# Two more blocks of seven products in a float32 transformer kernel: the per-layer gate's last two units, and the final norm in two halves

## The reference

```python
    y = _rms(h, norm_ple_g[i])
    h = h + jax.nn.sigmoid(y @ w_ple_gate[i]) * (p[i] @ w_ple_proj[i])
return _rms(h, final_norm_g)
...
x = x + swa_sink_mixer(rms_norm(x, swa_norm[idx]), swa_w_in[idx], ...)
```

## Time and profile before

| | |
|---|---|
| median of 3 runs | 1376.66 us (1376.61 to 1378.14) |
| the profiled execution | 1376.73 us |
| its span, first to last instruction | 1375.0 us |
| PE busy | 1369.3 us, 6169 instructions |
| DVE busy | 1156.1 us (84%) |
| ACT busy | 885.2 us (64%) |
| POOL busy | 151.3 us (11%) |
| mean granted TensorE clock | 1.000 |

### The profile page before, as it was taken

The page is one execution under the profiler, slowest core; times in us unless marked ns, Lnnn a source line. Parts: engine busy times, 40 slices in busy tenths (PEclk is TensorE's granted clock), DMA queues, the critical chain, the costliest instruction groups (busy, mean ns, idle before and its releaser), DMA issues.

```text
span 1375.0 us, 16935 instructions
## 1 busy us (share of the span) xinstructions
PE 1369.3 (100%) x6169; PEld 1122.6 (82%) x6169; DVE 1156.1 (84%) x1332; ACT 885.2 (64%) x1181; POOL 151.3 (11%) x129
## 2 busy tenths in 40 slices
PE   9999999999999999999999999999999999999998
PEld 7888888888888888888888888888888887777887
DVE  5589986687999988899999889988766769886898
ACT  7476755576777555777756576756666656665554
POOL 2000010011111000111100011100000144430000
PEclk9999999999999999999999999999999999999999
DMA  9776648887999788999987889998987878889686
GB/s 329 252 212 216 201 158 283 278 242 241 296 279 261 234 257 253 271 269 265 281 262 251 254 253 244 284 290 241 310 312 270 278 242 260 257 265 281 210 251 174
DMA packets 183146, 352.93 MB, mean 257 GB/s; under 512 B 13105, under 2 KB 37933, under 8 KB 182936
## 3 DMA queue, kind: packets, MB, share of 16 engines
q1 hardware_dynamic: 160408, 291.66, 64.5%
q0 software_dynamic: 9568, 35.02, 13.2%
q10 hardware_dynamic: 13088, 25.18, 6.1%
HBM read 296.19 MB, written 27.31 MB: 235 GB/s over the span
## 4 chain that ended last, share of the span: by engine, by line
PE 99%; DVE 0%; DMA 0%; ACT 0%; issue 0%; SPq 0%
PE acc L2216 14%; PE acc L2397 14%; PE acc L2400 14%; PE acc L2399 14%; PE acc L2217 14%; PE acc L2218 14%; PE sp L2400 2%; PE sp L2399 2%; PE tp L2400 2%; PE tp L2399 2%; PE sp L2397 2%; PE tp L2397 2%; PE acc L2278 1%; PE sp L2517 1%; PE tp L2533 1%; PE tp L2236 0%
## 5 line engine op out<-in xcount | busy, mean ns | idle before, releaser
L979 ACT ACTIVATE w_hi<-w_raw 128x1024 fp32r<-128x1024 f32 x451 | 472.1, 1056 | 294.8 <-PE acc L2218 188.0
L1419 DVE TENSOR_TENSOR w_lo<-w_raw,w_hi 128x1024 fp32r<-128x1024 f32 x429 | 519.1, 1225 | 131.6 <-ACT w_hi L979 128.7
L2216 PE MATMUL acc<-w_lo,hh 128*128 128x512 f32 x480 | 189.0, 394 | 0.0
L2218 PE MATMUL acc<-w_hi,hl 128*128 128x512 f32 x480 | 186.9, 389 | 0.0
L2217 PE MATMUL acc<-w_hi,hh 128*128 128x512 f32 x480 | 186.9, 389 | 0.0
L2397 PE MATMUL acc<-w_lo,yh 128*128 128x512 f32 x452 | 176.0, 389 | 0.0
L2399 PE MATMUL acc<-w_hi,yh 128*128 128x512 f32 x452 | 175.9, 389 | 0.0
L2400 PE MATMUL acc<-w_hi,yl 128*128 128x512 f32 x452 | 175.9, 389 | 0.0
L979 ACT ACTIVATE w_hi<-wide 128x1024 fp32r<-128x1024 f32 x108 | 114.3, 1060 | 69.6 <-DVE wide L1433 30.2
L1419 DVE TENSOR_TENSOR w_lo<-wide,w_hi 128x1024 fp32r<-128x1024 f32 x108 | 131.5, 1222 | 14.9 <-ACT w_hi L979 14.6
L2216 PE MATMUL acc<-w_lo,yh 128*128 128x512 f32 x352 | 137.4, 390 | 0.0
(11 more groups left out here) (333 smaller groups left out, 2227.6 us busy)
## 6 DMA issues: line engine op xcount, KB each, us to landing
w_raw<-in_w_gate SPq DMA_DIRECT2D x88, 512.0 KB, 5.8
w_raw<-in_w_up SPq DMA_DIRECT2D x88, 512.0 KB, 6.2
w_raw<-in_w_down SPq DMA_DIRECT2D x88, 512.0 KB, 6.4
w_raw<-in_w_in SPq DMA_DIRECT2D x64, 512.0 KB, 4.6
wide<-w_raw POOLq DMA_DIRECT2D x54, 512.0 KB, 5.9
w_raw<-in_swa_w_in ACTq DMA_DIRECT2D x48, 512.0 KB, 5.2
w_raw<-in_w_out SPq DMA_DIRECT2D x32, 512.0 KB, 5.8
w_raw<-in_w_ple_gate SPq DMA_DIRECT2D x32, 512.0 KB, 6.6
```

The source lines that it names most:

```text
L979: act.activation(w_hi[:, v % SPL], src, ACT.Copy).then_inc(hi_ready, 1)
L1419: dve.tensor_tensor(w_lo[:, v % SPL], src, w_hi[:, v % SPL].bitcast(F32), ALU.subtract).then_inc(lo_ready, 1)
L2216: pe.matmul(dst, xh[:, f, tk], w_lo[:, v % SPL, k], start=(f == 0), stop=False)
L2218: last = pe.matmul(dst, xl[:, f, tk], w_hi[:, v % SPL, k], start=False, stop=(f == CK * end + CK - 1))
```

## The change

Units 2 and 3 of the per-layer gate become one block (`PLE_PAIR`) with twenty entries: twelve plain chunks and two sets of `g`, `u`, `t`, `s`, for chunks 0 and 1 of both units. Its activation sums are made in the earlier part of the stage (`p_whole_sum`, `sum_p`, their high part on ACT, their low part on DVE). The sums of weights lie in `p_weights`, over parts of `hh` and `hl` that are not yet in use. The results of units 2 and 3 now come through DVE (`sum_third_gate` adds what `mix` left to the PSUM banks) and then through the sigmoid (`gate_third`). The loads of the projection are issued earlier. The moves of the first two columns to the second layer (`T_SWA`, `T_SWA + 1`) are both issued after the block's tenth load; before, one load and two further loads stood ahead of them. `SWA_STEPS` now takes four chunks of unit 0, four of unit 1, then the rest. The final norm's two instructions are set at two different chunks, each counted by itself.

```diff
-UNITS += [(8, "a")] * 4
+UNITS += [(8, e) for e in "aadd"]
...
-PLE_ORDER += [(j, c) for j in (2, 3) for c in range(8)]
...
+PLE_PLAN = plain(0, 2, 3) + quad("g", 0) + plain(0, 4) + quad("g", 1) + plain(0, 5) + plain(1, 2, 3) + quad("u", 0)
+PLE_PLAN += quad("t", 0) + quad("s", 0) + quad("u", 1) + plain(1, 4) + quad("t", 1) + quad("s", 1) + plain(0, 6, 7)
+PLE_PLAN += plain(1, 5, 6, 7)
+PLE_AT = dict(taken=(1, 3), turned=(2, 4), low=(7, 12), m1=13, mix=16, sum=18, pool_low=17,
+              copied={3: [0], 4: [1]}, summed={0: 7, 1: 11})
+PLE_PAIR = Block(PLE_UNIT + 2, PLE_PLAN, **PLE_AT)
...
-                if n in (13, 16, 19, 22):
-                    fetch_proj((13, 16, 19, 22).index(n))
-                if n == 26:
+                if n in (11, 14):
+                    fetch_proj((11, 14).index(n))
+            b = PLE_PAIR
+            for i, p in enumerate(b.loads):
+                role = int(p[0] == "u" or p[:2] == ("n", 1))
+                load(b.raw + i, wpg_v, CK * p[-1], CW * (2 + role))
+                if i in (4, 8):
+                    fetch_proj((4, 8).index(i) + 2)
+                if i == 9:
                     move(T_SWA, freed=T_PLE + 2)
-                if n == 28:
                     move(T_SWA + 1, freed=T_PLE + 3)
...
+            b = PLE_PAIR
+            for i in range(len(b.plan)):
+                for q in b.at["copied"].get(i, ()):
+                    copy_tops(b, q)
+                split_high(b.v0 + i)
+                if i in b.at["taken"]:
...
+                    take(PLE_UNIT + j, tok(0), ACT.Sigmoid, rp)
+                if i in b.at["turned"]:
...
+                    square(3, j, junk=1)
+                if i in b.at["low"]:
+                    swa_turned_high(b.at["low"].index(i))
+                if i == b.at["m1"]:
+                    copy_m1(b)
...
+            b = PLE_PAIR
+            for i in range(len(b.plan)):
+                if i != b.at["pool_low"]:
+                    split_low(b.v0 + i)
+                if i in b.at["taken"]:
+                    add_gated(b.at["taken"].index(i))
+                if i in b.at["turned"]:
+                    turn_gated(b.at["turned"].index(i))
+                if i in b.at["low"]:
+                    swa_turned_low(b.at["low"].index(i))
+                if i == b.at["mix"]:
+                    mix(b)
+                if i == b.at["sum"]:
+                    sum_third_gate(0)
...
-                        for t in range(T):
-                            last = dve.scalar_tensor_tensor(resid[:, t], resid[:, t], rs[:, R_FIN, t:t + 1], big[:],
-                                                            ALU.mult, ALU.mult)
-                        last.then_inc(x1_ready, 1)
...
+                        dve.scalar_tensor_tensor(resid[:, c], resid[:, c], rs[:, R_FIN, c:c + 1], big[:],
+                                                 ALU.mult, ALU.mult).then_inc(x1_ready, 1)
```

More of the change, by code:

```diff
@@ L335, in build @@
             h_wide_front = first.enter_context(nc.sbuf_tensor("h_wide", [P, PAIRS_OF_DOWN, 4, P], F32))
+        with ExitStack() as first:
+            p_weights = []
+            for i in range(2):
+                first.enter_context(nc.sbuf_tensor(f"front{i}", [P, 8, S], F32))
+                p_weights.append(first.enter_context(nc.sbuf_tensor(f"p_weights{i}", [P, 4, CW], F32)))
         hh, hl = sb("hh", [P, KT, S], F32R), sb("hl", [P, KT, S], F32R)
```

149 lines of the change are left out of this document (98 added, 51 removed).

## The result

The changed kernel took 1381.41 us (median of 7 runs, 1380.30 to 1382.71), the kernel before, run beside it, 1376.88 us (7 runs): a ratio of 1.0027, 95% interval 1.0017 to 1.0037. It is slower, by 4.5 us between the medians, where 1.5 us were forecast. The median lies 0.6 us above the end of the forecast range (1380.8); the ratio, laid on the 1376.66 us of before, gives 1380.4, just inside. The profiled execution is the longest of the seven, 1382.71 us, 5.98 us over the profiled one of before.

The account below looks back on a forecast made before the run. PE was taken to bound the kernel, so every matmul removed and every PE wait counts: 1376.73 - 1.36 (six matmuls) + 2.8 (waits in the block) = 1378.2 us. The range was 1375.3 to 1380.8.

Parts of the forecast that it names:

- Six matmuls, -1.36 us: In the block, two sets of 21 matmuls replace 2 x 24, six fewer at 0.2267 us each: 1.36 us less.
- First place, sixth entry, 0.7: At the block's sixth entry, DVE's split is ready at 1028.45, wanted at 1027.8; PE waits about 0.7 us.
- Second place, the load at the thirteenth entry: The load waits for raw slot and SP's list, landing at 1039.2; PE starts at 1041.7 instead of 1040.0.
- The accumulating transfer is no limit: issued at about 1021.1, landed 5.9: POOL's transfer for the sums, in the block: landed 5.9 us after issue, wanted only past 1030, so no wait.
- Third place, `t` 1: At the fourteenth entry, the second column's parts stand between splits; PE starts at 1045.5 instead of 1042.8.
- The three places together, 2.8: Waits at the block's sixth, thirteenth and fourteenth entries together make PE 2.7 to 2.8 us late; 2.8 taken.
- The projection's earlier loads ... nothing, and at worst the 1.2 us of one instruction: First half of the stage: earlier projection loads and activation sums cost nothing, at worst 1.2 us.
- the 8.0 us of the slowest load in the stage: Loads behind the thirteenth entry's: even at 8.0 us to landing their chunks are in time.
- all first loads behind a fetch stayed at 5.0 or less: Argument against the late-load rival: first loads behind a fetch landed in 5.0 us or less.
- The second layer at nothing: Second layer's start: third and fourth columns and the final norm in halves are in time; cost nothing.
- The rival of a late load: Thirteenth entry's load lands in up to 8.0 us, fourteenth entry 6.1 us late, time 1381.5; chance 0.12.
- The quick load: Thirteenth entry's load lands at 1037.5, fourteenth entry only 1.1 us late, time 1376.5; chance 0.13.

Follow-up runs that it names:

- e2: Changed kernel with ACT's two copies for the sums of weights at the block's first and third entries, not fourth and fifth; 3.29 us of waits in the block.
- e3: Changed kernel with the second column's high and low parts at the block's fifteenth entry instead of its thirteenth, behind `s` 1; median 1383.00 us.
- n1: The kernel before with only its final norm in two halves; stage 87.04 us, rest to the last matmul 310.70 us.
- e1: Changed kernel with the projection's four fetches back where they stood before; median 1381.35 us against 1381.41.
- e4: Changed kernel with three loads between the two column moves, as before the change; median 9.3 us over that of the changed kernel.
- e11: e10 with the bias rows' loads back behind GpSimd's scale for the second layer; times 1376.36 to 1382.32 us.
- e5: Changed kernel with both first-pair sets behind five plain products and the moves behind the eleventh and twelfth loads; stage 88.95 us.
- e10: e9 with the keys' last two products ahead of the second unit's chunk 4; stage 86.96 us, rest 310.69 us, one run at 1375.99.
- e9: e6 with bias rows issued ahead of POOL's next scale and the sums' copies one entry earlier; stage 86.29 us.
- e6: e5's order and moves, plus earlier copies, low parts at `(7, 16)` and projection fetches as before, on the changed kernel; stage 86.47 us, time same as before.

## Why the prediction was wrong in its size

The side and the kind of mechanism were right: slower, with waits that eat the gain of the six matmuls. The size was not, 4.5 us for 1.5; the forecast had given a time above 1379.4 a chance of 0.16. By its steps:

- *Six matmuls, -1.36 us*: right; 186 matmuls in the block.
- *First place, sixth entry, 0.7*: 0.77, and gone with earlier copies (e2).
- *Second place, the load at the thirteenth entry*: right in place, cause and landing (4.6 for 4.7), but 2.43 us where 1.0 were forecast. It failed in one step, the sentence "The accumulating transfer is no limit: issued at about 1021.1, landed 5.9". I asked only when that transfer itself is wanted. What it does to the fetch beside it I left at the rows of a stretch without one: 2.7 us a piece became 6.2. That puts the high part, the last sum, the slot and so the load some 2.2 us later, and makes a wait before `t` 0 that stood nowhere in the walk. The trace of before had a row that could have warned me, the fetch issued at 975.75 us, beside a transfer of 1024 KB from POOL's queue:

```profile
tile<-parked SPq DMA_DIRECT2D x4, 128.0 KB, 6.6
```

- *Third place, `t` 1*: 1.07 us for 1.1, and its cause as forecast (e3).
- *The three places together, 2.8*: 4.89 us in the changed kernel, 3.29 in e2, where no accumulating transfer is beside the fetch. The 3.29 are near 2.8 in part by luck, with one put 1.0 us longer and the other 1.6 us shorter than the 4.2 priced.
- *"The projection's earlier loads ... nothing, and at worst the 1.2 us of one instruction"*: 1.7 us of wait before unit 2 in the profile of the changed kernel, none there in the four others with that order. I looked for cover on DVE and ACT and not in the DMA queue, though the row that it rests on has a DMA share of 0.98. That step is incomplete in any case: the fetch took 8.9 to 13.9 us for 5.3 to 6.8, and only the column's slack hid it from PE in four of five.
- *"the 8.0 us of the slowest load in the stage"* and *"all first loads behind a fetch stayed at 5.0 or less"*: both misread. In the trace of before a load issued at 982 us took 11.4, and the load of 8.0 us, issued at 978.30, is itself the first behind a fetch. The result does not hang on it, since the load in question took 4.6.
- *The second layer at nothing*: right for the columns and for the cutting of the norm in halves (2.35 us each at 1084.20 and 1087.60, no late split; n1). Wrong for `SWA_STEPS` and for the norm's later place, which holds up the bias rows: 0.42 us together. I asked when the inputs come and not who waits for the first unit's result.
- *The rival of a late load*, 1381.5 us, met the time, but not by its mechanism: it has a slow landing of the load (up to 8.0 us), which took 4.6. *The quick load*, on the side of the page "DMA: Bandwidth & Descriptors" of the Trainium skill (section "Anatomy of one DMA — SWDGE (gpsimd) path"), is out: the loads behind the second fetch landed in 4.6 us (after) and 4.7 (e2). By the page's line an estimate for 512 KB is 3.2 us; that line is given for transfers that GpSimd issues, and these are SP's.

## What to carry to other kernels

When a change adds a transfer or moves one forward, price what it does to every transfer that is in the air with it, not only whether it is itself in time; if the DMA engines' share is near 1 there, expect it to take longer itself and others to come later, and look whether their slack holds. Where a load is held by a slot and by a queue, taking one away shows the other; giving the slot to an entry wanted later helps against both. A written order that ends a unit one product later is late for the chain behind that unit, however well its inputs are covered. And before a gap seen in one profile is put down to an edit, look for it in the profiles of the other kernels that have the same order there.

## What the runs showed of the hardware

- A gap can cost more than its length, because TensorE's clock may fall behind it. In e1, PE's timeline behind its gap at the thirteenth entry:

```profile
1046.06 0.50 PE L2494 MATMUL acc<-w_lo,yh 128*128 128x512 f32 x1 [2.19 <-DVE w_lo L1463]
...
1047.60 0.63 PE L2494 MATMUL acc<-w_lo,yh 128*128 128x512 f32 x1
1048.03 0.63 PE L2496 MATMUL acc<-w_hi,yh 128*128 128x512 f32 x1
...
1050.96 0.39 PE L2497 MATMUL sp<-w_hi,y_sums_lo 128*128 128x512 f32 x1
```

  The starts are 0.43 us apart instead of 0.227 from 1047.6 to 1050.6, seven or eight matmuls, some 1.6 us, and the granted clock of the window from 1046 to 1051 is 0.66 (columns as in the earlier trace rows):

```profile
1046.00:1051.00 5.00, 4.94 (x15) 3.86 (x16) 4.12 (x6) 4.97 (x7) 0.00 (x0) 0.66 0.60 179
```

  That is the lower level, 1.2 GHz, for part of it. In e4 the same stood behind its gap of 2.67 us and again behind that of 6.75, and in e11 behind the 2.15 us of idle time before the scores (granted clock 0.66 from 1128 to 1133); e11's rest is 3.8 us longer than that of before, where the gap by itself is worth 2.2. In the profiles of after, e2 and e3, PE was idle for 2.16, 1.91 and 2.07 us at the same entry, and the clock stayed at 2.4 GHz. So it comes in some executions and not in others behind nearly the same gap. That the times of kernels with such waits scatter more may come of it. The forecast had the clock stay, and in the profile of after it did.
- A fetch of four pieces of 128 KB takes longer when an accumulating transfer of 512 KB from SBUF to SBUF is issued within 1.3 us of it: 6.2, 6.1, 6.2, 6.1 and 5.8 us a piece in after, e1, e3, e4 and e5. It took 2.7 in before and in e2, 2.7 and 2.8 in e10 and e9, and 3.1 in e6, where that transfer had been issued 4.7 us ahead.
- The first matmul of 512 columns behind a wait is 0.30 to 0.35 us ahead of its follower, where one in a row is 0.227: some 0.1 us more. That holds for 24 waits of 0.2 us and more in these traces; two others, in e4, have the lower clock behind them.
